# A hybrid decoder trunk on one Trainium2 core: decay differences and decay squares on ScalarE, cumulative sums spread in split format

## The reference, cut to what matters

```
cum = cumsum(dt * A)                      # per head, along the chunk
seg = cum[t] - cum[s]
decay = exp(where(t >= s, seg, -inf))
cb = C[t] . B[s]
y_intra = sum_s cb[t,s] * decay[t,s] * dtx[s]
```

```
log_a = -8 * r * softplus(-lam);  a = exp(log_a)
mult = sqrt(-expm1(2 * log_a));  u = mult * (i * xc)
h[t] = a[t] * h[t-1] + u[t]
```

## Time and profile before

| | us |
|---|---|
| median of 3 runs | 1759.11 |
| lowest and highest | 1756.7, 1759.35 |
| the profiled execution | 1762.06 |
| its span | 1760.3 |

### The profile page before, as it was taken

How to read it: one execution, slowest core, us unless ns; L and a number is a source line. 1 busy time by engine, 2 the same in 40 slices (tenths; PEclk the granted TensorE clock), 3 DMA queues, 4 the chain that set the end, 5 groups by cost and what they waited for, 6 DMA issues and landing times.

```text
span 1760.3 us, 24065 instructions
## 1 busy us (share of the span) xinstructions
PE 1710.1 (97%) x8992; PEld 1440.2 (82%) x8992; DVE 1356.7 (77%) x1376; ACT 1055.5 (60%) x1013; POOL 112.3 (6%) x117
## 2 busy tenths in 40 slices
PE   7999999999999999999999999999999999999996
PEld 5877899999887789888788788788788788787885
DVE  3678766664357876688888888888888988888886
ACT  2535544433243554677777776776776766777675
POOL 2054000000105400000000000000000000000000
PEclk9999999999999999899999999999999999999999
DMA  8455354646545535499899899899899999998993
GB/s 254 144 179 180 130 173 144 187 134 180 184 132 172 189 122 190 153 362 359 316 367 354 315 363 358 322 360 351 324 358 333 346 357 322 356 360 309 368 359 111
DMA packets 257159, 465.51 MB, mean 264 GB/s; under 512 B 8492, under 2 KB 108196, under 8 KB 257056
## 3 DMA queue, kind: packets, MB, share of 16 engines
q1 hardware_dynamic: 250736, 443.28, 72.8%
q0 software_dynamic: 6064, 20.19, 3.3%
q10 hardware_dynamic: 288, 1.08, 0.2%
HBM read 453.70 MB, written 11.15 MB: 264 GB/s over the span
## 4 chain that ended last, share of the span: by engine, by line
PE 87%; DVE 7%; ACT 3%; issue 2%; POOL 0%; DVEq 0%; ACTq 0%; POOLq 0%
PE bank L884 84%; PE bank L888 3%; DVE arena L1783 2%; DVE w_lo L1786 1%; ACT w_hi L1414 1%; ACT arena L1414 1%; DVE moe_rows L1783 1%; DVE fw_lo L1786 1%; ACT fw_hi L1414 1%; DVE cs_t L1786 0%; DVE arena L1786 0%; DVE sam_y L1875 0%; DVE ysb_lo L1783 0%; DVE bank L1997 0%; DVE rs L1786 0%
## 5 line engine op out<-in xcount | busy, mean ns | idle before, releaser
L1786 DVE TENSOR_TENSOR w_lo<-wring,w_hi 128x2048 fp32r<-128x2048 f32 x336 | 768.4, 2291 | 109.7 <-ACT w_hi L1414 108.9
L1414 ACT ACTIVATE w_hi<-wring 128x2048 fp32r<-128x2048 f32 x336 | 644.4, 1920 | 250.4 <-PE bank L884 250.3
L884 PE MATMUL bank<-w_hi,xg_hi 128*128 128x512 f32 x896 | 357.4, 399 | 13.6 <-DVE w_lo L1786 12.1
L884 PE MATMUL bank<-w_hi,xg_lo 128*128 128x512 f32 x896 | 353.5, 395 | 0.0
L884 PE MATMUL bank<-w_lo,xg_hi 128*128 128x512 f32 x896 | 352.4, 393 | 0.0
L884 PE MATMUL bank<-hn,wring 128*128 128x264 f32 x1152 | 269.1, 391 | 8.5 <-DVE hn L1783 6.1
L884 PEld LDWEIGHTS bank<-hn,wring 128*128 128x128 f32 x1152 | 218.6, 192 | 51.5 <-issue 11.7
L884 PEld LDWEIGHTS bank<-w_hi,xg_hi 128*128 128x128 f32 x896 | 168.3, 188 | 54.7 <-DVE w_lo L1786 13.7
L884 PEld LDWEIGHTS bank<-w_lo,xg_hi 128*128 128x128 f32 x896 | 168.4, 188 | 38.1
L884 PEld LDWEIGHTS bank<-w_hi,xg_lo 128*128 128x128 f32 x896 | 168.5, 188 | 36.2
L884 PE MATMUL bank<-w_hi,at_hi 128*128 128x512 f32 x448 | 177.9, 397 | 1.8 <-DVE at_lo L1786 1.8
(11 more groups left out here) (261 smaller groups left out, 2055.4 us busy)
## 6 DMA issues: line engine op xcount, KB each, us to landing
wring<-in_moe_w_gate SPq DMA_DIRECT2D x112, 1024.0 KB, 5.7
wring<-in_moe_w_up SPq DMA_DIRECT2D x112, 1024.0 KB, 5.5
wring<-in_moe_w_down SPq DMA_DIRECT2D x112, 1024.0 KB, 5.3
wring<-in_w_in SPq DMA_DIRECT2D x36, 1024.0 KB, 5.3
wring<-in_w_out SPq DMA_DIRECT2D x16, 1024.0 KB, 5.2
wring<-in_ffn_w_gate SPq DMA_DIRECT2D x11, 1024.0 KB, 5.5
wring<-in_ffn_w_up SPq DMA_DIRECT2D x11, 1024.0 KB, 5.4
wring<-in_ffn_w_down SPq DMA_DIRECT2D x16, 704.0 KB, 4.7
```

What stands on the lines that cost most here:

```text
L884: return nc.tensor.matmul(out, lhsT, rhs, start=start, stop=stop)
L1414: return nc.scalar.activation(out, in_, fn, **kw)
L1786: return V.tensor_tensor(out, in0, in1, op)
```

## The change

- `cum` is spread as two products per head in split format (fp32r): `cum_parts` holds the rounded high part and the remainder of `dts[:, CUM]`, `head_id` is the fp32r copy of the identity. ACT writes the high part at m = 5 of the xl phase, DVE the low part there.
- The differences move from DVE to ACT: four Relu of 128x128 on the PSUM tile, with scale -1 and bias cum[s], then the Exp with scale -1. Relu(cum[s] - cum[t]), negated, is min(cum[t] - cum[s], 0).
- `rg*rg` moves from DVE to ACT: one Square of 128x528, after the two Exp of its pair. The buffer `rs` is single, so that the Square of pair k waits until DVE has used pair k-1.

```
@@ PE, gate phase
                     out = begin("cum", l, m)
+                    pe.wait_ge(cum_ready, l + 1)
                     for i in range(2):
                         h = 2 * m + i
-                        ins = mm(out[:, i * TP:(i + 1) * TP], ident[0:HEADS, h:h + 1].to_broadcast([HEADS, P]),
-                                 dts[:, CUM, 0:TP])
+                        for part in range(2):
+                            ins = mm(out[:, i * TP:(i + 1) * TP], head_id[:, h:h + 1].to_broadcast([HEADS, P]),
+                                     cum_parts[:, part, :], start=part == 0, stop=part == 1)
@@ ACT, xl phase
+                    if m == 5:
+                        evacuated("cb", l)
+                        act.wait_ge(sbc_ready, 2 * l + 2)
+                        f(cum_parts[:, 0, :], dts[:, CUM, 0:TP]).then_inc(cum_hi_ready, 1)
@@ ACT, gate phase
                     if m > 0:
+                        cums = filled("cum", l, m - 1)
+                        for i in range(2):
+                            for c in range(NC):
+                                v = cums[:, i * TP + c * Q:i * TP + (c + 1) * Q]
+                                h = 2 * (m - 1) + i
+                                ins = f(v, v, ACT.Relu, scale=-1.0, bias=tok[:, 3 * c + 1, h:h + 1])
+                        ins.then_inc(seg_diff, 1)
                         act.wait_ge(seg_diff, 8 * l + m)
-                        diff = bank[fill("cum", l, m - 1)[0]][:, :]
-                        f(diff, diff, ACT.Exp).then_inc(segexp_ready, 1)
+                        f(cums[:, :], cums[:, :], ACT.Exp, scale=-1.0).then_inc(segexp_ready, 1)
...
+                        if pair:
+                            act.wait_ge(lru_exp, XT * l + 2 * m)
+                            if m > 1:
+                                act.wait_ge(square_used, (XT // 2 - 1) * l + m - 1)
+                            f(rs[:, 0:2, :], rg[:, pair[0]:pair[1] + 1, :], ACT.Square).then_inc(decay_squared, 1)
@@ DVE
+            V.tensor_copy(head_id[:, :], ident[0:HEADS, 0:HEADS])
@@ DVE, lru_factors
-                dve.wait_ge(lru_exp, XT * l + 2 * k + 2)
-                link(tt(rs[:, 0:2, :], rg[:, two, :], rg[:, two, :], ALU.mult))
-                ins = stt(th[:, two, :], rs[:, 0:2, :], 1.0, th[:, two, :], ALU.add, ALU.mult)
-                if k < XT // 2 - 1:
-                    link(ins)
-                else:
-                    ins.then_inc(mult_arg, 1)
+                dve.wait_ge(decay_squared, XT // 2 * l + k + 1)
+                stt(th[:, two, :], rs[:, 0:2, :], 1.0, th[:, two, :], ALU.add, ALU.mult
+                    ).then_inc(square_used if k < XT // 2 - 1 else mult_arg, 1)
@@ DVE, xl phase
+                    if m == 5:
+                        dve.wait_ge(cum_hi_ready, l + 1)
+                        tt(cum_parts[:, 1, :], dts[:, CUM, 0:TP], cum_parts[:, 0, :].bitcast(F32), ALU.subtract
+                           ).then_inc(cum_ready, 1)
@@ DVE, gate phase
-                    if m < XT:
-                        out = filled("cum", l, m)
-                        for i in range(2):
-                            h = 2 * m + i
-                            for c in range(NC):
-                                v = out[:, i * TP + c * Q:i * TP + (c + 1) * Q]
-                                ins = V.tensor_scalar(v, v, tok[:, 3 * c + 1, h:h + 1], 0.0, ALU.subtract, ALU.min)
-                        ins.then_inc(seg_diff, 1)
```

More of the change, by code:

```diff
@@ L305, in trunk @@
         diag = sb("diag", [HEADS, HEADS])
+        head_id = sb("head_id", [HEADS, HEADS], F32R)
         tok = sb("tok", [P, 7, HEADS])
@@ L404, in trunk @@
         fw = [[ffn(f"fw_{part}{i}", UNIT) for part in ("hi", "lo")] for i in range(FSLOTS)]
+        cum_ctx = ExitStack()
+        cum_ctx.enter_context(nc.sbuf_tensor("cum_place", [P, dtxe_at + NC * HEADS * HD + XT * T - 4 * FSLOTS * UNIT // 2], F32))
+        cum_parts = cum_ctx.enter_context(nc.sbuf_tensor("cum_parts", [HEADS, 2, TP], F32R))
+        cum_ctx.close()
         out_ctx = ExitStack()
@@ L500, in trunk @@
         dt_ready = sem("dt_ready")
+        cum_hi_ready = sem("cum_hi_ready")
+        cum_ready = sem("cum_ready")
         dec_ready = sem("dec_ready")
@@ L507, in trunk @@
         mult_arg = sem("mult_arg")
+        decay_squared = sem("decay_squared")
+        square_used = sem("square_used")
         mult_ready = sem("mult_ready")
```

## The result

| kernel | median of its runs, us | lowest and highest | runs |
|---|---|---|---|
| before | 1756.77 | 1753.97 to 1761.69 | 7 |
| after | 1749.66 | 1748.72 to 1750.09 | 7 |

After is to before as 0.9948, interval 0.9933 to 0.9963: 7.1 us less. The forecast was 1754.3, 4.8 us less, with a range down to 1751.2. Sign and order of size are right, and the time lies 1.5 us under the range. The changed kernel's profiled execution took 1749.19 us, 12.87 less than the one before. That is more than the medians show, and the rest of this document is mostly about why.

A forecast was written before the change was run, and what follows sets the result against it. PE, busy 97%, and in the gate phases a DVE-POOL ring were the bounds; -2.4 us per layer, -4.8 in all, took 1762.06 to 1757.3, less 2.95 gives 1754.3; range 1751.2 to 1759.3, likeliest case 1752.7 to 1756.9.

The forecast's parts named there:

- The hold: Gate phases: DVE's `ig` waits for POOL's second product and ends 0.58 us after it, 2.96 us instead of 0.70.
- the ring: Gate phases, from DVE step 3: state update, POOL's two products, `ig`, `rg*rg`, `th`; 8.36 us a turn, 7.6 after.
- The differences: Four per step on DVE, 1.04 us, run while POOL holds up `ig`: moving them gains nothing in the ring.
- the squares: `rg*rg` with its wait leaves DVE: 0.73 us less in each of steps 3, 4 and 5.
- cum tiles: PE's spread of cum in split format: 0.65 us per tile instead of 1.06, saving 0.41.
- pacemaker of the first tiles: Early gate tiles: ACT needs 6.85 us per tile against PE's 6.64, so only 0.2 us per tile is won.
- Square 3: ACT's Square would wait some 3 us for DVE's `th`, hidden by 2 us.
- Rival (c): Relu not in Tanh and Exp's table: two 1.28 us loads per block, +19 us in both layers, 1778; chance 0.05.
- Rival (b): ACT bounds the whole stretch, with Relu about 0.55 us: gain only 1.4 us, 1757.7; chance 0.15.
- The gate phase: Per layer, `mult_arg` and the start of z tile 1 come 2.35 us earlier: 0.15 + 3 x 0.73.
- My "0.15" for the entry: State update of step m = 2, ahead of the ring, comes 0.1 to 0.2 us early.
- all that follows are PE's and move with it: After z tile 1, `intra`, z 2 and the rest shift earlier with it: -2.4 us per layer.

The follow-up runs named there:

- `square_only`: The kernel before with only the decay's Square moved to ACT (fp32 spread, differences on DVE): 0.9985 of the kernel before.
- `pe_square`: The changed kernel without the Relu (differences back on DVE): 0.9947 of the kernel before, median 1749.7; repeated, 0.9969, median 1751.78.
- `after_pool`: The changed kernel with POOL's two products cut to one row of eight in six of eight chunks per layer: 0.9938 of the kernel before, median 1748.76.

## Why the prediction was right in mechanism and missed the time

**Right.** The hold is real: `ig` still ends 0.57 us past POOL's products, two updates are 7.62 apart against the 7.6 forecast (in part luck: the turn ahead of it is 7.46, and the 7.62 contains POOL's wait for its load), and cutting POOL's products short frees 1.4 to 1.6 us per layer. The Trainium skill, "SBUF — State Buffer", section "Who interferes with whom", says that a VectorE instruction with two SBUF inputs contends with a GpSimd instruction that reads SBUF; the trace agrees (3.62 us beside POOL's products, 0.70 without). The differences were worth nothing in the ring (its turn is 7.44 to 7.47 in `square_only`, with them on DVE, and 7.46 after), the squares some 0.7 to 0.9 a turn, cum tiles took 0.65, ACT became the pacemaker of the first tiles, Square 3 stood 3.08 us unseen. Rival (c) did not happen: no table load at any Relu. Here the Trainium skill, "ScalarE: Activation LUTs", section "Table sets: the hidden batching unit" (relu in every set), agrees with the trace. Its rule that gives relu to VectorE, up to three times faster in bf16, is not borne out by the speed of the two engines here: in fp32 on PSUM four Relu take ACT 1.11 us and the four differences take DVE 1.13. `pe_square`, without the Relu, is 0.7 and 0.9 us a layer shorter in its first trace and 0.3 and 0.5 longer in its second. Rival (b) needed a Relu of 0.55 us; one lasts 0.35.

**Mis-sized.** The gate phase: 2.78 measured, 2.35 forecast. Most of the 0.43 is in how early the ring is entered: the update of step 2 comes 0.44 us earlier, not 0.15. Behind it are ACT's tiles, 6.64, 6.74 and 6.76 us from one pair's gate Tanh to the next instead of 6.85, with a Relu block of 1.14 instead of 1.23. The turns then save 0.88, 0.69 and 0.74 where I had three times 0.73, and PE waits 0.53 instead of 0.9 before z tile 1. My "0.15" for the entry was the difference of two estimates of a microsecond. In both layers it is 0.8 us; the likeliest case's own range (1752.7) had room for it.

**The step that failed** is the one that turned phases into a time: "the profiled execution would go from 1762.06 to 1757.3. The median of the runs lies 2.95 below that execution; the same difference taken from it gives 1754.3." That takes the 2.95 for a constant offset. It is none: the changed kernel's profiled execution lies 0.47 us below the median of its runs, not 2.95 above. The times of before are a mixture, with medians of 1754.5 and 1761.6 in its two groups, 7 us apart, and the execution I read was one of the slower sort; three runs with a median of 1759.11 hid that. Taken from the upper group's median, 1754.5, the same -4.8 would have given 1749.7. That it would have come so close to the 1749.66 measured is partly luck, since the gate phases gave 5.56.

With it fails "all that follows are PE's and move with it": it is PE's, but its length depends on the granted clock: the run-up took 19.1 us with 0.50 in it, and 14.9 at 1.00. Had I seen the 0.50 in 711 to 718, which the trace of before had plainly, the sum would have had a term of its own. In the upper group the runs go from 1754.5 to 1749.1, 5.3 less, against 5.56 in the gate phases and 4.8 forecast. The other 1.8 us of the measured 7.1 lie in which executions were drawn: the seven runs of before have one at 1753.97, three round 1756.7, two round 1759.2 and one at 1761.69, while all seven of after lie within 1.4 us with a mean clock of 0.995 or more.

**Open.** What decides in which execution the clock falls ahead of the experts, and why the start of the program takes 1.9 us more in one execution than in another. Shifts of 2.75, 5.5 and 11 us, in either layer, came with a mean clock of 0.993 or less in a quarter to three quarters of the runs, and the kernel before shows both groups with no edit at all. Whether it is the position of that work in time, or how much PE did before it, the runs do not separate: the one edit that took work away made PE wait instead. So whether the changed kernel would keep its 11 of 13 on other days is not shown. That the wait for the store of the state chunks lengthens the ring's turn is read from the traces, where the two go together to 0.01 us; no edit that shortens this wait was run, and what makes the store late is open.

## What to carry to other kernels

Before an operation is moved off a busy engine, ask which barrier it runs ahead of: work that fills the time until another engine lets go is worth nothing, and the same microsecond inside the ring is worth its full length in every turn, until another chain round the same turn is the longer one. A part that shortens only PE's list can make the kernel longer, as here, where PE then stood still for 3.17 us and its next products ran at the lower clock; test parts in the combination in which they will run. And before a sum is taken off a median, look at the spread of the runs and at the granted clock of each stretch of the trace: two groups of runs are two kernels to predict.

## What the runs showed of the hardware that I had not expected

- A single standstill of PE of 3.17 us was followed by sixteen matmuls in 5.52 or 6.89 us instead of 3.83, one of 2.33 by 5.51 in one layer and, at 2.32, by 3.83 in the other; behind 1.21, 0.53 and 0.48 us it was 3.83 each time.
- The granted clock can also fall while PE is busy without a gap: 7.00 of 7.00 us busy in 704 to 711, then 0.50 in 711 to 718, in some executions of a kernel and not in others.
- VectorE's wait covers both of two GpSimd instructions in a row (1.91 + 2.35), also where it arrives in the first: it did not get in between them.
- Low parts on DVE paid the same price out of the ring: the subtraction for `cum_parts` (16 x 256) takes 2.94 us beside POOL's products, and 0.40 in `after_pool`. It was hidden: PE's first cum tile after, at 115.50, comes 10.6 us behind its end. DVE's timeline after:

```profile
101.95 2.94 DVE L1812 TENSOR_TENSOR cum_parts<-dts,cum_parts 16x256 fp32r<-16x256 f32 x1
```
